# Sixteen key pages of the sample attention asked for on SyncE at the prompt attention's last scores, four more into a room of their own

## The chip, the core and the metric

The kernel runs on one core of a Trainium2 chip. The core has five engines with a queue of instructions each: PE (TensorE, matmuls and transposes), DVE (VectorE), ACT (ScalarE), POOL (GpSimd) and SP (SyncE, which here only issues DMAs), and 16 DMA engines that carry what the queues ask for. PEld is the load of a matmul's stationary operand. The metric is the device time of one execution in microseconds, the median of several; lower is better.

## The reference, cut to what matters

One step of a two-layer decoder for two groups of tokens that share all weights: a prompt of 512 tokens and a sample of 8 sequences with one new token each. The change touches one part of layer 0, the attention of the sample.

```
def nsa_sample(xn, kv_cmp_pages, kv_sel_pages, kv_win_buf, page_table, ...):
    past = page_table.shape[1] * PAGE_SIZE             # 8 pages of 128 rows, 1024 keys
    ...
    def gather_past(pages):
        return pages[page_table].reshape(b, past, 2, N_KV_HEADS, HEAD_DIM)
    ...
    sel_all = jnp.concatenate([gather_past(kv_sel_pages), sel_new], axis=1)
    win_all = jnp.concatenate([kv_win_buf, jnp.stack([k_w, v_w], axis=2)], axis=1)
    ...
    o = nsa_attend(q, q_rot, gates, pos, kc, vc, sel_blk[:, :, :, 0], sel_blk[:, :, :, 1],
                   win_all[:, :, 0], win_all[:, :, 1], kw_pos)
```

Each of the 8 sequences has 8 pages of selected-branch keys and 8 of values (a page is 128 rows of 256 f32, 128 KB), found through `page_table`, and one window of 512 keys and 512 values (512 KB each). Nothing of what is computed changes.

## The kernel before

The program is a row of blocks. At the end of a block every engine drains, reports to a barrier, and goes on when all five have reported; the instructions of the next block start behind it. Two neighbouring blocks matter.

**The prompt attention** (L2357 and on) works in units n = 0 to 39: scores on PE, exponents, scaling, transposes and products with the values. SP has nothing to compute there. It issues DMAs for the block that follows, each group behind a wait on how far the prompt attention has come (`scored`, `o_filled`, `c_turned`), because the rooms come free one after another.

**The sample attention** (`stage_sample_attention`, L2836 and on) takes the keys in 12 groups g of four transposed tiles: `group(n)` gives for turn n the parity j of the sequence, the part (2 is the window, 0 and 1 are the first and last four pages), the half a and the quarter q, so that the sequence is b = 2q + j. Groups 0 to 5 are the even sequences, 6 to 11 the odd ones. Each turn is four transposes into PSUM, a copy to `sa_kT`, and one of four products; the semaphore `turned` counts turns. Before group 8 PE waits for part 0 of the odd sequences, before group 10 for part 1 (`k_landed`). Then come softmax steps, and the products with the values (L2956), first for sequences 0 to 3 (bg = 0), then 4 to 7 (bg = 1); before each half PE waits for `v_landed` of its four sequences.

The values are loaded by `rows_values`, 9 DMAs a sequence (the window and 8 pages). Most land in rooms that keys held before, so they wait for `turned` to reach 8, 24, 32, 40 or 48 (`v_free`). SP loads sequences 0, 1, 4, 5; POOL 2, 3, 6, 7. Behind its last value page SP asks for the first weight tile of the next stage (`load_first_weights`, L2697, 2 MB into `w_first`).

A page's number comes from the table in SBUF. SP has read the numbers of its own sequences 0, 1, 4, 5 into registers before (`read_table`). For the other four, `early_keys` has SP read the number at the page (`table`, L2744: a TENSOR_LOAD and two register operations ahead of the DMA). Below, such a page is a table page, the other kind an own page.

The key pages of the odd sequences, `k_slots(1, part, q)`, are loaded so before: (1, 0, q=0) by SP at the end of the prompt attention; (1, 0, 2), (1, 1, 0), (1, 1, 2) by SP and (1, 0, 1), (1, 0, 3), (1, 1, 1), (1, 1, 3) by POOL at the start of the sample attention.

Of the kernel before, what the change touches and what calls it, by code (L numbers as in the profile page):

```python
# [19 lines left out]
P = 128  # L20
# [10 lines left out]
KVW = NKV * HD  # L31
# [56 lines left out]
class Core:  # L88


    def __init__(self, nc, ctx, dram):
        self.nc, self.ctx, self.dram, self.sems = nc, ctx, dram, []
        self.psum = ctx.enter_context(nc.psum_tensor("psum", [P, 8, 512], F32))
# [38 lines left out]
def columns(w):  # L132

    view = w.rearrange("(k p) n -> p k n", p=P)
    return lambda g, chunk: view[:, chunk * CK:(chunk + 1) * CK, g * NG:(g + 1) * NG]
# [2132 lines left out]
def stage_prompt_attention(c, cache):  # L2268
# [20 lines left out]
    scaled, turned = ([c.sem(f"att_{x}_{par}") for par in ("even", "odd")] for x in ("scaled", "turned"))  # L2289
    kept = [c.sem(f"att_kept_{half}") for half in ("first", "second")]  # L2290
    o_filled, o_kept = c.sem("att_o_filled"), c.sem("att_o_kept")
    with ExitStack() as mine:
# [64 lines left out]
        with nc.Block() as block:  # L2357
# [264 lines left out]
            @block.sync  # L2622
            def _(sp):
                cache.read_table(sp, "sp")
                sp.wait_ge(c.h_stored, 16)
                cache.first_selected(sp)
                sp.wait_ge(k_turned, 4)
                cache.first_windows(sp)
                sp.wait_ge(scored, 2 * NR)
                cache.window_keys(sp, 1, 0, 0)  # L2630
                sp.wait_ge(o_filled, 4)
                cache.early_keys(sp, 0, 1, 2, 0, 2)
                sp.wait_ge(scored, 4 * NR)
                cache.window_keys(sp, 1, 1, 1)
                sp.wait_ge(o_filled, 8)
                cache.early_keys(sp, 0, 1, 2, 2, 4)
                sp.wait_ge(c_turned, 3)
                cache.early_keys(sp, 0, 1, 0, 0, 4)
                cache.early_keys(sp, 0, 1, 1, 0, 2)
                sp.wait_ge(scored, 6 * NR)  # L2640
                cache.window_keys(sp, 1, 2, 0)
                sp.wait_ge(o_filled, 12)
                cache.early_keys(sp, 0, 1, 3, 0, 2)
                sp.wait_ge(c_turned, 4)
                cache.early_keys(sp, 0, 1, 1, 2, 4)
                sp.wait_ge(scored, NU)
                cache.window_keys(sp, 1, 3, 1)
                cache.early_keys(sp, 1, 0, 0, 0, 4)


NKC = PAST // P
# [43 lines left out]
def load_first_weights(c, sp):  # L2695

    sp.dma_start(c.w_first[:], columns(c.dram["nsa_w_o"][0])(0, 0)).then_inc(c.w_first_landed, 16)  # L2697


class SampleCache:  # L2700
# [5 lines left out]
    def __init__(self, c):  # L2706
        self.c, self.values = c, {}
        self.sel_pages = c.dram["cache_kv_sel"][0].rearrange("g t s h d -> g t (s h d)")
        self.win = c.dram["cache_kv_win"][0].rearrange("b (c t) s h d -> b t c (s h d)", t=P)
        self.k_landed = [[[c.sem(f"sa_k_landed_{j}_{part}_{e}") for e in ("sp", "pool")] for part in range(3)] for j in range(2)]  # L2710
        self.v_landed = [c.sem(f"sa_v_landed{b}") for b in range(NB)]
        self.kept_h = c.hT[:].rearrange("p k t -> p (k t)")[:, 0:16 * KVW].rearrange("p (s x) -> p s x", x=KVW)
        self.more = None

    def dead(self, q):

        row, half = ((0, 0), (0, 1), (1, 0), (2, 0))[q]
        return self.c.kv[:, 0:QT, row, half * KVW:(half + 1) * KVW]

    def k_slots(self, j, part, q):  # L2720

        if j == 0 and part == 2:
            return self.dead(q)
        if j == 0 and part == 0:
            return self.kept_h[:, 4 * q:4 * q + 4]
        at = 16 * {(0, 1): 0, (1, 2): 1, (1, 0): 2, (1, 1): 3}[j, part] + 4 * q
        return self.more[:, at:at + 4]

# [66 lines left out]
def stage_sample_attention(c, cache):  # L2795
# [11 lines left out]
    turned, kept, scored, s_done = c.sem("sa_turned"), [c.sem("sa_kept_act"), c.sem("sa_kept_dve")], c.sem("sa_scored"), c.sem("sa_scores_done")  # L2807
# [4 lines left out]
    with ExitStack() as mine:  # L2812
# [23 lines left out]
        with nc.Block() as block:  # L2836
            @block.sync
            def _(sp):
                cache.early_keys(sp, 0, 1, 3, 2, 4)
                cache.keys(sp, 1, 0, 2)  # L2840
                for q in (0, 2):
                    cache.keys(sp, 1, 1, q)
                for b in cache.OWN["sp"]:
                    cache.rows_values(sp, b, turned)
                load_first_weights(c, sp)

            @block.gpsimd
            def _(pool):
                for part in range(2):
                    for q in (1, 3):  # L2850
                        cache.keys(pool, 1, part, q)
                for b in cache.OWN["pool"]:
                    cache.rows_values(pool, b, turned)

# [1195 lines left out]
```

## Time and profile before

| | us |
|---|---|
| median of 3 runs | 1504.61 |
| lowest, highest | 1503.66, 1506.21 |
| the profiled execution, its own time | 1503.56 |
| its span, first to last instruction | 1501.9 |
| prompt attention ends (last PE instruction ends) | 397.0 |
| sample attention, PE's first to last instruction | 398.0 to 463.3 |

The span is read as a chain: PE is busy 97% of it, so a microsecond comes off the end only if PE loses it. The sample attention is one of the few places where PE has gaps that other engines or transfers decide. Times in the rows are from the start of the span. "Idle before" is how long the engine stood before an instruction, and the name behind the arrow is what released it; "issue" stands where the profile shows no releaser. A q behind an engine's name is its sequencer, which runs waits, register and DMA-issuing instructions.

### The profile page before, as it was taken

The numbers are of one execution on the slowest core, as the hardware profiler recorded it, in microseconds if no ns is written. First come the engines' busy times: TensorE is split into PE (matmuls) and PEld (weight loads), VectorE is DVE, ScalarE is ACT, GpSimd is POOL, SyncE is SP. The second block draws the span as 40 slices with busy tenths as digits, with TensorE's granted clock in tenths as the row PEclk, the third lists the DMA queues.
The fourth block names the chain that finished last, engine by engine and source line by source line (L and its number), as shares of the span: only waits on it lengthen the run. The fifth ranks groups of instructions, "written<-read, shape, count | busy, mean of one in ns | idle before, by whom it ended". The sixth has DMA issues, their size and how long they took to land. (4 is left out here: it accounts for less than half of the span.)

```text
span 1501.9 us, 25637 instructions
## 1 busy us (share of the span) xinstructions
PE 1459.0 (97%) x9697; PEld 1216.4 (81%) x9697; DVE 867.1 (58%) x1878; ACT 418.0 (28%) x1052; POOL 353.7 (24%) x478
## 2 busy tenths in 40 slices
PE   8999999899999999999999999899999999999998
PEld 7877799655557888888888888688888888888888
DVE  2755344788555795654767725661585556776513
ACT  3011333788520533324200001442531111000012
POOL 0000300467640369991000036380000000000000
PEclk9999999999999999999999999999999999999999
DMA  8345472221496445363344311602312222322201
GB/s 271 116 126 150 128 235 63 80 71 44 149 350 157 156 166 168 134 228 138 120 135 133 110 63 55 282 31 92 108 61 81 88 98 71 113 84 84 85 28 58
DMA packets 142893, 184.34 MB, mean 123 GB/s; under 512 B 31299, under 2 KB 101643, under 8 KB 141747
## 3 DMA queue, kind: packets, MB, share of 16 engines
q1 hardware_dynamic: 139634, 174.31, 35.4%
q0 software_dynamic: 3136, 8.39, 1.7%
q8 instruction: 77, 1.26, 0.3%
q14 instruction: 46, 0.37, 0.1%
HBM read 163.42 MB, written 29.69 MB: 129 GB/s over the span
## 5 line engine op out<-in xcount | busy, mean ns | idle before, releaser
L2619 POOL TENSOR_SCALAR att_p<-att_p,att_tot,gates 128x128 f32<-128x128 f32 (+3 forms) x128 | 79.1, 631 | 45.2 <-DVE att_tot L2541 44.6
L296 PE MATMUL psum<-xT,l_w 128*128 128x260 f32 x384 | 85.3, 383 | 2.0 <-PEq L113 1.8
L953 PE MATMUL psum<-xT,l_w 128*128 128x260 f32 x384 | 85.2, 383 | 1.6 <-PEq L113 1.6
L296 PEld LDWEIGHTS psum<-xT,l_w 128*128 128x128 f32 x384 | 72.8, 190 | 13.5 <-issue 2.4
L953 PEld LDWEIGHTS psum<-xT,l_w 128*128 128x128 f32 x384 | 72.8, 190 | 12.9 <-issue 1.8
L969 PE MATMUL psum<-l_up_t,l_w_sums 128*128 128x260 f32 x336 | 78.2, 382 | 0.0
L2145 PE MATMUL psum<-cmp_xt,cmp_w 64*128 64x256 f32 (+1 forms) x640 | 72.2, 362 | 0.3 <-DVE cmp_xt L2066 0.3
L969 PEld LDWEIGHTS psum<-l_up_t,l_w_sums 128*128 128x128 f32 x336 | 63.8, 190 | 9.8
L2592 ACT ACTIVATE att_p<-att_p,att_low 128x128 f32<-128x128 f32 (+3 forms) x128 | 70.4, 553 | 2.7 <-DVE att_low L2532 2.7
L1232 ACT ACTIVATE l_hidden<-l_tmp 128x260 f32<-128x260 f32 x64 | 26.6, 420 | 144.9 <-DVE l_tmp L1382 144.9
L2532 DVE CUSTOM_DVE_ANT_0 att_p<-psum,causal 128x128 f32<-128x128 f32 (+3 forms) x128 | 55.8, 487 | 18.7 <-PE psum L2367 17.9
L312 PE MATMUL psum<-xT,l_w 128*128 128x260 f32 x272 | 62.9, 382 | 0.0
L969 PE MATMUL psum<-xT,l_w 128*128 128x260 f32 x272 | 62.9, 382 | 0.0
L312 PE MATMUL psum<-l_up_t,l_up_w_sums 128*128 128x260 f32 x264 | 61.5, 382 | 0.0
L2145 PEld LDWEIGHTS psum<-cmp_xt,cmp_w 64*128 64x128 f32 x640 | 60.7, 187 | 0.6 <-DVE cmp_xt L2066 0.5
L969 PE MATMUL psum<-xT,l_w_sums 128*128 128x260 f32 x256 | 60.4, 382 | 0.0
L969 PEld LDWEIGHTS psum<-xT,l_w 128*128 128x128 f32 x272 | 51.7, 190 | 7.9
L1086 PE MATMUL psum<-l_hidden,l_w 128*128 128x260 f32 (+2 forms) x384 | 58.1, 311 | 0.0
L1715 PE MATMUL psum<-xT,proj_w 128*128 128x260 f32 x256 | 56.8, 383 | 0.7 <-DMA proj_w<-in_nsa_w_in 0.5
L312 PEld LDWEIGHTS psum<-xT,l_w 128*128 128x128 f32 x272 | 51.1, 190 | 7.5
L1086 PEld LDWEIGHTS psum<-l_hidden,l_w 128*128 128x128 f32 x384 | 53.8, 191 | 3.9
L455 PE MATMUL psum<-l_hidden,l_w 128*128 128x260 f32 x256 | 56.4, 382 | 0.0
(584 smaller groups left out, 3148.8 us busy)
## 6 DMA issues: line engine op xcount, KB each, us to landing
l_w<-in_mlp_w SPq DMA_DIRECT2D x16, 2048.0 KB, 8.0
l_w<-in_mlp_w SPq DMA_DIRECT2D x32, 1024.0 KB, 5.1
proj_w<-in_nsa_w_in SPq DMA_DIRECT2D x4, 2048.0 KB, 10.3
cmp_raw<-in_cache_kv_cmp SPq DMA_DIRECT2D x24, 256.0 KB, 3.0
xT<-in_cache_kv_cmp SPq DMA_DIRECT2D x24, 256.0 KB, 3.0
sa_more<-in_cache_kv_sel POOLq DMA_DIRECT2D x44, 128.0 KB, 6.6
sa_more<-in_cache_kv_sel SPq DMA_DIRECT2D x34, 128.0 KB, 8.0
hT<-in_cache_kv_cmp SPq DMA_DIRECT2D x16, 256.0 KB, 3.1
```

The lines of the kernel that those rows point to most:

```text
L296: mm = nc.tensor.matmul(ps[:, n % 8, 0:HALF], w[s][:, k, m * P:(m + 1) * P], src[:, kk, cols(h)], start=(kk == 0), stop=(kk == last))
L312: mm = nc.tensor.matmul(ps[:, bank, 0:HALF], left(k), right(k), start=(fresh and k == 0), stop=(ends and k == KC - 1))
L455: mm = nc.tensor.matmul(ps[:, LAST_BANKS[h, m], 0:HALF], wt[:, k, at:at + P], hid[:, kk, cols(h)], start=(kk == 0), stop=(kk == KF - 1))
L953: mm = nc.tensor.matmul(ps[:, n % 8, 0:HALF], w[s][:, k, m * P:(m + 1) * P], src[:, kk, cols(h)], start=(kk == 0), stop=(kk == last))
L969: mm = nc.tensor.matmul(ps[:, bank, 0:HALF], left(k), right(k), start=(fresh and k == 0), stop=(ends and k == KC - 1))
L1086: mm = nc.tensor.matmul(ps[:, LAST_BANKS[part][m], 0:width(part)], wt[:, k, at:at + P], hid[:, kk, PARTS[part]], start=(kk == 0), stop=(kk ...
L1232: nc.scalar.activation(hid[:, tile, cols(h)], tmp[:, i % 4], ACT.Square).then_inc(hid_done, 1)
L1715: mm = nc.tensor.matmul(ps[:, bank_of(step), 0:HALF], w[:, j, k, m * P:(m + 1) * P], c.xT[:, k, h * HALF:(h + 1) * HALF], start=(k == 0), ...
L2145: mm = nc.tensor.matmul(out, w1[z * HD:(z + 1) * HD, i % 2, t].rearrange("p r e -> p (r e)"), moving, start=(t == 0), stop=(t == STRIDE - 1))
L2532: nc.vector.tensor_tensor_reduce(pr[:, n % PR, par, at:at + w], ps[:, score_bank(n, par), at:at + w], c.causal[:, SEQ - w:SEQ], 1.0, 3e38, ...
L2592: nc.scalar.activation(pr[:, n % PR, par, at:at + w], pr[:, n % PR, par, at:at + w], ACT.Exp, scale=-1.0, bias=low[:, n % PR, u, par:par + ...
L2619: ve.tensor_scalar(pr[:, n % PR, par, at:at + w], pr[:, n % PR, par, at:at + w], tot[:, n % PR, u, par:par + 1], c.gates[:, i, gate:gate + ...
```

## The change

Three things.

At the end of the prompt attention SP asks for 16 pages, (1, 0, q) for q = 0, 2, 1, 3 behind the wait for the last scores, where it asked for the four of q = 0. And it asks near the block's start for the four pages of (1, 1, 0), into a new room `sa_spare`.

In the sample attention SP then has only (1, 1, 2) of the odd keys left, four pages in place of twelve, and POOL eight in place of sixteen.

`sa_spare` lies partly on `w_first`, so SP waits for `turned` to reach 45 (the last reading of the room) before it asks for the weight tile.

```
@@ first_windows, in the prompt attention @@
                 cache.first_windows(sp)
+                cache.early_keys(sp, 1, 1, 0, 0, 4)
                 sp.wait_ge(scored, 2 * NR)
...
                 sp.wait_ge(scored, NU)
                 cache.window_keys(sp, 1, 3, 1)
-                cache.early_keys(sp, 1, 0, 0, 0, 4)
+                for q in (0, 2, 1, 3):
+                    cache.early_keys(sp, 1, 0, q, 0, 4)
@@ SampleCache @@
+        self.spare = c.place("sa_spare", [P, 4, KVW], 222112 - 55488)
...
+        if (j, part, q) == (1, 1, 0):
+            return self.spare[:]
@@ stage_sample_attention, SP @@
                 cache.early_keys(sp, 0, 1, 3, 2, 4)
-                cache.keys(sp, 1, 0, 2)
-                for q in (0, 2):
-                    cache.keys(sp, 1, 1, q)
+                cache.keys(sp, 1, 1, 2)
                 for b in cache.OWN["sp"]:
                     cache.rows_values(sp, b, turned)
+                sp.wait_ge(turned, 45)
                 load_first_weights(c, sp)
@@ POOL @@
-                for part in range(2):
-                    for q in (1, 3):
-                        cache.keys(pool, 1, part, q)
+                for q in (1, 3):
+                    cache.keys(pool, 1, 1, q)
```

How this moves instructions, in the words of the built programs (a DMA row names what it fills and from what; ISA is the register work of the page's address; three or more like rows are cut to "..."):

SP, end of the prompt attention, before: four own pages, then the end of the block (L2357) and the barrier.

```order
L2762 DMA sa_early<-in_cache_kv_win 128x4x256 [waits att_scored]
L2780 ISA
L2780 DMA sa_early<-in_cache_kv_sel 128x256
...
L2357 UNCONDITIONAL_BRANCH
L2837 UNCONDITIONAL_BRANCH [waits barrier_Pool_Activation_PE_DVE_SP_release]
```

The same place in the changed program (L2785 is the old L2780, L2749 the old L2744): eight own pages (q = 0, 2), then eight that read the table first (q = 1, 3).

```order
L2767 DMA sa_early<-in_cache_kv_win 128x4x256 [waits att_scored]
L2785 ISA
L2785 DMA sa_early<-in_cache_kv_sel 128x256
...
L2749 TENSOR_LOAD pages
L2749 ISA x2
L2785 ISA
L2785 DMA sa_early<-in_cache_kv_sel 128x256
...
L2357 UNCONDITIONAL_BRANCH
L2842 UNCONDITIONAL_BRANCH [waits barrier_Pool_Activation_PE_DVE_SP_release]
```

Between the last scores and SP's report to the barrier now stand 16 page DMAs and 8 table reads, where there were 4 page DMAs.

SP, end of the sample attention, before: the weight tile straight behind the last value page.

```order
L2792 ISA [waits sa_turned]
L2792 DMA sa_more<-in_cache_kv_sel 128x256
...
L2697 DMA l_w_49<-in_nsa_w_o 128x8x512
L2836 UNCONDITIONAL_BRANCH
L235 UNCONDITIONAL_BRANCH [waits barrier_Pool_Activation_PE_DVE_SP_release]
```

And in the changed program:

```order
L2797 ISA [waits sa_turned]
L2797 DMA sa_more<-in_cache_kv_sel 128x256
...
L2699 DMA l_w_49<-in_nsa_w_o 128x8x512 [waits sa_turned]
L2841 UNCONDITIONAL_BRANCH
L235 UNCONDITIONAL_BRANCH [waits barrier_Pool_Activation_PE_DVE_SP_release]
```

The weight tile has a wait of its own now; nothing else stands behind it on SP in this block.

## Rows read from the trace of the kernel before

**Rows 1.** The page: busy time, share of the span, instructions.

```profile
PE 1459.0 (97%) x9697; PEld 1216.4 (81%) x9697; DVE 867.1 (58%) x1878; ACT 418.0 (28%) x1052; POOL 353.7 (24%) x478
```

**Rows 2.** Timeline of PE, 395 to 466 us: start, length, what, idle before.

```profile
395.90 1.13 PE L2412 MATMUL psum<-qT,attc_vcz 128*128 128x512 f32 x2
397.96 0.65 PE L2865 MATMUL psum<-kcs,qz 128*32 128x63 f32 x32 [0.93 <-PEq L2357]
...
405.93 1.99 PE L2887 MATMUL psum<-ident,hT 128*128 128x128 f32 x16
407.90 1.06 PE L2897 MATMUL psum<-sa_kT,qz 128*32 128x512 f32 x8
...
441.62 1.09 PE L2922 MATMUL psum<-ident,qz 128*128 128x128 f32 x8 [1.89 <-DVE qz L3004]
...
449.52 0.39 PE L2956 MATMUL psum<-sa_more,sa_kT 128*16 128x256 f32 x2
451.31 0.62 PE L2956 MATMUL psum<-vcs,causal 63*16 63x256 f32 x8 [1.40 <-issue]
...
465.08 35.30 PE L296 MATMUL psum<-xT,l_w 128*128 128x260 f32 x160 [1.75 <-PEq L113]
```

**Rows 3.** Instructions of L2357, the barrier at the prompt attention's end: duration, start.

```profile
L2357 SPq DRAIN  x1: 122/122/122, 388.3 to 388.3; - x1
L2357 POOLq DRAIN  x1: 2282/2282/2282, 389.6 to 389.6; - x1
L2357 ACTq DRAIN  x1: 614/614/614, 397.1 to 397.1; - x1
```

**Rows 4.** Waits of SP's queue, 285 to 399 us: total, times, longest.

```profile
SPq L2357 <- PEq L2357: 9.4, 1, 9.4
```

**Rows 5.** Timeline of SP, 285 to 399 us.

```profile
296.56 2.08 SPq L2762 DMA_DIRECT2D kv<-in_cache_kv_win  x4
300.42 0.37 SPq L2762 DMA_DIRECT2D sa_early<-in_cache_kv_win  x1
317.01 0.89 SPq L2780 DMA_DIRECT2D sa_early<-in_cache_kv_sel  x2
...
374.49 3.96 SPq L2780 DMA_DIRECT2D sa_early<-in_cache_kv_sel  x4
385.78 0.39 SPq L2762 DMA_DIRECT2D sa_early<-in_cache_kv_win  x1
386.36 1.91 SPq L2780 DMA_DIRECT2D sa_early<-in_cache_kv_sel  x4
```

**Rows 6.** SP's page DMAs, 386 to 389 us (four own pages): duration, first and last start.

```profile
L2780 SPq DMA_DIRECT2D sa_early<-in_cache_kv_sel x4: 333/333/368, 386.4 to 387.9; - x4
```

**Rows 7.** SP's table reads, 347 to 352 us (two), then 373 to 379 us (four).

```profile
L2744 SPq TENSOR_LOAD <-pages x2: 265/269/273, 349.5 to 350.6; - x2
...
L2744 SPq TENSOR_LOAD <-pages x4: 267/268/276, 373.8 to 377.4; - x4
L2744 SPq FUSED_REGOPS  x4: 152/154/159, 374.1 to 377.7; - x4
```

**Rows 8.** Page DMAs of L2759, SP (eight own, eight table pages), first and last start.

```profile
L2759 SPq DMA_DIRECT2D hT<-in_cache_kv_sel x16: 332/333/651, 283.2 to 296.2; - x16
```

**Rows 9.** Windows: us, busy of five engines, granted clock, DMA share, GB/s.

```profile
392.00:396.00 4.00, 4.00 (x43) 2.22 (x41) 0.69 (x1) 0.58 (x1) 0.00 (x0) 1.00 0.00 0
408.00:412.00 4.00, 4.00 (x34) 2.15 (x34) 2.09 (x4) 1.26 (x3) 3.13 (x6) 1.00 1.06 354
448.00:452.00 4.00, 2.60 (x48) 1.09 (x44) 1.68 (x4) 0.00 (x0) 0.00 (x0) 1.00 1.07 371
```

**Rows 10.** Page DMAs of L2792 in tile `sa_more`: all of SP; then SP, POOL from 430 us.

```profile
L2792 SPq DMA_DIRECT2D sa_more<-in_cache_kv_sel x20: 333/654/1489, 408.2 to 441.3; - x20
...
L2792 POOL DMA_DIRECT2D sa_more<-in_cache_kv_sel x15: 537/537/877, 429.9 to 442.2; - x15
L2792 SPq DMA_DIRECT2D sa_more<-in_cache_kv_sel x13: 333/416/1315, 429.9 to 441.3; - x13
```

**Rows 11.** Timeline of POOL, 411 to 462 us.

```profile
428.66 0.76 POOL L2789 DMA_DIRECT2D sa_more<-in_cache_kv_win  x1 [4.55 <-PE psum L2887]
...
435.02 2.32 POOL L2792 DMA_DIRECT2D sa_more<-in_cache_kv_sel  x4 [3.44 <-PE psum L2887]
...
438.08 4.67 POOL L2792 DMA_DIRECT2D sa_more<-in_cache_kv_sel  x8
```

**Rows 12.** DMAs in issue 442.6 to 443 us: count, KB each, us to landing.

```profile
l_w<-in_nsa_w_o SPq DMA_DIRECT2D x1, 2048.0 KB, 13.9
sa_more<-in_cache_kv_sel SPq DMA_DIRECT2D x1, 128.0 KB, 9.9
sa_more<-in_cache_kv_sel POOLq DMA_DIRECT2D x1, 128.0 KB, 7.2
```

**Rows 13.** DMA queues, 444 to 446 us: packets, MB, share.

```profile
q1 hardware_dynamic: 192, 0.18, 29.2%
q0 software_dynamic: 191, 0.52, 76.7%
```

**Rows 14.** Windows around a gap of PE in the prompt attention, columns as rows 9.

```profile
278.00:280.00 2.00, 0.31 (x4) 0.00 (x0) 1.93 (x7) 1.74 (x9) 1.50 (x2) 1.00 0.00 0
280.00:281.00 1.00, 0.73 (x2) 0.47 (x4) 1.00 (x8) 1.00 (x5) 0.00 (x0) 0.67 0.00 0
281.00:283.00 2.00, 2.00 (x20) 1.12 (x16) 2.00 (x6) 1.04 (x5) 1.91 (x3) 0.50 0.00 0
283.00:284.00 1.00, 0.60 (x6) 0.38 (x4) 1.00 (x3) 0.97 (x2) 0.78 (x2) 0.62 0.00 0
```

**Rows 15.** Timeline of PE, 276 to 294 us.

```profile
280.27 2.04 PE L2367 MATMUL psum<-att_kT,qrT 64*128 64x512 f32 x4 [1.96 <-DVE att_low L2532]
...
287.83 1.13 PE L2367 MATMUL psum<-att_kT,qrT 64*128 64x512 f32 x4 [2.56 <-DVE att_low L2532]
```

## The prediction

> **What bounds the kernel now.** I read the page's busy times first: PE is busy 97% of the span [rows 1], so only what PE loses or wins counts. Then PE's timeline through the two blocks that the change touches [rows 2]. Between the prompt attention and the sample attention PE stands 0.93 us, released by the barrier. The twelve groups of key turns are back to back: a group of 16 transposes and its products takes 1.99 + 1.06 us less a little overlap, 405.93 to 408.90, and the next ones look alike, none with a wait for a transfer. So the keys that the change asks for earlier keep nobody waiting now. Two gaps follow: 1.89 us for a DVE chain, and 1.40 us at 449.91 before the first product of bg = 1, put down to "issue". For that gap I looked at the transfers, since PE waits there for `v_landed` of sequences 4 to 7. SP's last value page was asked for at 441.3 [rows 10] and landed 9.9 us later [rows 12], at 451.2; PE goes on at 451.31. POOL's last page was asked for at 442.2 and landed 7.2 us later, at 449.4. So the 1.40 us belong to SP's pages of sequence 5, which sat in a full queue: the DMA engines carry about 350 GB/s without a pause there [rows 9]. Last I looked at who reaches the barrier when [rows 3]: SP drains at 388.3 and stands 9.4 us [rows 4]; ACT is the last, its drain ends at 397.1 + 0.61 = 397.7.
>
> **What the change removes.** Sixteen pages of 128 KB, 2.1 MB, leave the sample attention, 2.1 / 350 GB/s = 6.0 us of transfer. SP's value pages no longer stand behind eight key pages. The last eight wait for `turned` = 40, which POOL's row dates at 428.66 [rows 11]; asked for at 0.5 us each they are out by 433 and, even at today's 9.9 us, in by 443. So SP's pages fall away as the reason for the gap. What is late next is POOL's last page. POOL's queue is unchanged from `turned` = 24 on: its last 13 DMAs still wait for `turned` = 48 and go out from 435.0 to 442.75 [rows 11]. With its 7.2 us it is in at 449.4, half a microsecond before PE asks. The gain is the whole 1.40 us. It cannot be more: before the gap PE runs without one from 441.62, behind it PE and DVE work on as before, and the next stage's first tile landed at 442.7 + 13.9 = 456.6 [rows 12], 8 us before its first product at 465.08 [rows 2].
>
> **What the change adds at the end of the prompt attention.** This is the term that decides. Behind the wait for the last scores (released at 385.78) SP had one window and four own pages, and was through at 388.3 [rows 5]. Now 12 more pages stand there, and the barrier behind them is one that PE waits for. An own page costs (387.9 − 386.4) / 3 = 0.51 us from start to start [rows 6]. A table page costs more: in the row at 374.49 four of them take 3.96 us; less the last DMA's own 0.33 that is 3.63 / 3 = 1.21 us [rows 5]. Rows 8 give a second value: 15 steps in 13.0 us, seven of them own, so (13.0 − 7 × 0.51) / 8 = 1.18. Two table reads in the middle of the block start 349.5 and 350.6, 1.1 us apart [rows 7]. I take 1.15, between the last and the other two. The additions are 4 × 0.51 + 8 × 1.15 = 2.0 + 9.2 = 11.2 us. SP's last DMA starts at 387.9 + 11.2 = 399.1, ends at 399.5, and its drain of 0.12 us at 399.6. The barrier would have opened at 397.7, so SP is now the last and PE, with everybody, starts the sample attention 1.9 us later. With 1.1 us a table page SP is done at 399.2 and 1.5 us late, with 1.21 at 400.1 and 2.4 late.
>
> A narrower reading is possible from the durations alone: a table read is 0.27 us and its register work 0.15 [rows 7], so a table page would be 0.51 + 0.44 = 0.95 us, SP done at 398.0 and 0.3 us late. I keep 0.3 as the lower bound and don't take it as the value, because the starts show a gap behind each read that no row accounts for. The Trainium skill (DMA: Bandwidth & Descriptors, "Latency and other measured facts") puts the floor of a `tensor_load` at about 600 ns. As an estimate by that page, a table page would be 0.51 + 0.60 = 1.11 us and SP 1.6 us late; the row's 0.27 us duration speaks against the page's figure, the distance of the starts for it.
>
> **The rest.** The four pages of (1, 1, 0) go out near the block's start, behind the kv windows (issued 296.56 to 298.64). They are own pages: 4 × 0.51 = 2.0 us to 300.7. The next DMA, now at 300.42, slips by 0.3 us, and SP's next wait ends at 317.0 [rows 5], so it costs nothing; without that pause it would cost 2.0. The 12 more pages at the end cross an idle DMA system (share 0.00 from 392 to 396 [rows 9]). POOL issues 8 key pages instead of 16 and then waits for `turned` = 8; nothing of its is on the path. The new wait for `turned` = 45 has nothing behind it on SP but the weight tile. PE passes 45 turns about 432, before SP is through with its value pages, so the tile goes out around 434 and not at 442.7. Its 2.1 MB now share the engines with POOL's last 2.1 MB. With at most 1.0 MB of sequence 5 still outstanding that is 5.2 MB / 350 GB/s = 15 us from 434.4, so everything is in by 449.4 at the latest, still before 449.9. All these times slide together with the late barrier.
>
> **The sum.** +1.9 (SP late at the barrier) − 1.4 (gap before bg = 1) = +0.5 us. Everything else is 0. The profiled execution would go from 1503.56 to 1504.1; it lies 1.05 us below the median, which is the execution's luck, so I add the difference to the median: 1504.61 + 0.5 = 1505.1.
>
> **Rivals.**
>
> B, SP is in time. Table pages at the end of the block cost 0.9 us or less: 8 × 0.9 + 2.0 ends SP at 397.6. Then only the gap goes: 1504.61 − 1.4 = 1503.2. For it: the durations [rows 7]. Against it: three stretches of SP's queue [rows 5, 7, 8].
>
> C, the pause lets TensorE's clock fall. PE's pause at the barrier grows from 0.93 to about 2.8 us. The trace has a pause of 1.96 us before 280.27 [rows 15] behind which the granted clock is 0.67, 0.50 and 0.62 (its lower level, 1.2 GHz, for the middle two) until 284 [rows 14]: 0.33 + 1.0 + 0.38 = 1.7 us of full clock lost. But behind the pause of 2.56 us before 287.83 nothing fell, and before this barrier PE has been busy without a pause for 5 us. If it falls: +0.5 + 1.7 = +2.2, 1506.8. The Trainium skill (TensorE: Matmul & The Clock Gate, "Part 1: The HAM clock gate") ties the level to how busy the engine has just been and halves the clock after idleness; the two pauses here show both outcomes.
>
> D, the gap stays. The weight tile takes the place of SP's pages beside POOL's. The two queues take turns by packet (192 against 191 packets [rows 13]), POOL's being the larger now, 0.52 against 0.18 MB; if the tile's packets are larger than page rows, POOL's share falls. POOL has half a microsecond to lose. Then the 1.4 us stay: +1.9, 1506.5. Against it: the 15 us bound above, and SP's queue being empty far earlier.
>
> E, the other side: SP is held up by a full queue. In the sample attention a page DMA takes 0.65 us in the median, 1.49 at most, instead of 0.33 [rows 10]. If the twelve added ones were held up so, SP would be 12 × 0.32 = 3.8 us later still: +0.5 + 3.8 = +4.3, 1508.9. It decides from the point where pages are asked for faster than they are carried, one in 0.37 us at 350 GB/s. Own pages come one in 0.51 us, table pages slower, so it should not.
>
> **How the numbers follow.** Forecast 0.58, B 0.10, C 0.14, D 0.12, E 0.06. The forecast's own range is 1503.5 (0.3 us late) to 1505.6 (2.4 late) by the bounds of the table page, and 1502.9 to 1506.5 with half the spread of the three runs of before (1503.66 to 1506.21). The range reaches to B's and D's times and a little past C: 1502.6 to 1507.2; E lies outside, with the edges of B and C. A measurement of this kernel tells about 0.2%, 3.0 us, from no change. Faster by that needs B and 1.6 us more: 0.03. Slower needs E, or C and D together: 0.08. Within: 0.89.
>
> **What would show it.** In the changed profile: SP's last page DMA before the barrier starts at 399.1 and its drain, not ACT's, is the last; POOL and ACT wait for it. PE's gap before L2868 (the old L2865) is about 2.8 us, not 0.93. The gap of 1.40 before the first product of bg = 1 is gone, and the products of bg = 0 and 1 follow each other. From the start of the sample attention to its last PE instruction it is 65.3 − 1.4 = 63.9 us. The granted clock stays at 1.00 in the windows from 400 on. The forecast is wrong if SP reaches the barrier before 397.7 (B), if the clock reads 0.5 behind the pause (C), if a gap remains in L2959 (D, the old L2956), or if page DMAs of L2785 last over 0.4 us at the block's end (E).

## The result: slower by 0.3%, and the profile after

The changed kernel takes 1508.55 us in the median of 10 runs (1505.91 to 1513.76); the kernel before, in 10 runs beside it, 1505.38 (1503.61 to 1507.79). The ratio is 1.0029 with a 95% interval of 1.0017 to 1.0041, that is 4.4 us (2.6 to 6.2). I had forecast +0.5 us, 1505.1, with a range up to 1507.2. A second set on another chip gave 1508.76 against 1505.17, ratio 1.0024 (1.0014 to 1.0034).

The profiled execution is one of the slowest: 1513.76 us, a span of 1512.1. So its 10.2 us over the profile before are not the change's price; its single steps are what can be read. PE's timeline in it, to be held against [rows 2] (start, length, what, idle before):

```profile
395.32 1.12 PE L2412 MATMUL psum<-qT,attc_vcz 128*128 128x512 f32 x2
399.63 1.07 PE L2868 MATMUL psum<-kcs,qz 128*32 128x63 f32 x32 [3.19 <-PEq L2357]
...
401.44 5.04 PE L2890 MATMUL psum<-ident,kv 128*128 128x128 f32 x24
...
446.07 1.16 PE L2925 MATMUL psum<-ident,qz 128*128 128x128 f32 x8 [1.89 <-DVE qz L3007]
...
447.37 1.05 PE L2959 MATMUL psum<-vcs,causal 63*16 63x256 f32 x8
...
459.06 0.62 PE L2959 MATMUL psum<-vcs,causal 63*16 63x256 f32 x8
```

Three things differ. PE's pause at the barrier is 3.19 us, it was 0.93. The transposes of the first six key turns take 5.04 us; in the kernel before they took 2.97:

```profile
399.07 2.97 PE L2887 MATMUL psum<-ident,kv 128*128 128x128 f32 x24
```

And bg = 0 of the value products takes 11.7 us (447.37 to 459.06), where it took 7.2 and a gap of 1.40. The barrier's own rows, against [rows 3] (duration, start), and what SP did before it, against [rows 5]:

```profile
L2357 ACTq DRAIN  x1: 616/616/616, 396.5 to 396.5; - x1
L2357 SPq DRAIN  x1: 123/123/123, 399.2 to 399.2; - x1
```

```profile
385.76 13.42 SPq L2785 DMA_DIRECT2D sa_early<-in_cache_kv_sel  x16
```

SP is the last now, done at 399.3 where ACT is done at 397.1: 2.2 us. The sixteen pages take 13.42 us. One of the first three is a page DMA that lasts 1.10 us instead of 0.33 (shortest, median and longest, first and last start):

```profile
L2785 SPq DMA_DIRECT2D sa_early<-in_cache_kv_sel x16: 332/333/1103, 385.8 to 398.9; - x16
```

Less these 0.77 us, the last DMA's 0.33 and seven own steps of 0.51 that is 8.75 / 8 = 1.09 us a table page. The windows of PE, against [rows 9] (us, busy of five engines, granted clock, DMA share, GB/s), say what the slow stretches are:

```profile
400.00:404.00 4.00, 4.00 (x104) 3.98 (x96) 1.33 (x5) 0.59 (x1) 3.47 (x7) 0.50 0.66 200
...
408.00:412.00 4.00, 4.00 (x36) 2.89 (x35) 1.88 (x3) 2.10 (x6) 2.88 (x5) 1.00 1.07 357
...
420.00:424.00 4.00, 4.00 (x34) 2.76 (x32) 1.58 (x3) 1.76 (x3) 2.78 (x5) 1.00 0.49 145
...
448.00:452.00 4.00, 4.00 (x40) 1.27 (x40) 0.84 (x3) 0.00 (x0) 0.00 (x0) 0.50 1.03 362
```

The granted clock is 0.50, the level of 1.2 GHz, behind the long pause and again behind the pause of 1.89 us. From 420 to 424 the DMA engines are half idle (share 0.49, 1.08 in the kernel before): with fewer keys to fetch, the queues have at that time nothing more to carry.

### The profile page after: what moved, and what is told of

It reads as the page before. It is cut to its first block and busy times, and to the rows that moved or that the text cites. A ratio compares the mean times of both kernels' runs of the same rounds, so it can differ in the third digit from the quotient of the medians.

```text
span 1512.1 us, 25661 instructions
## 1 busy us (share of the span) xinstructions
PE 1468.7 (97%) x9697; PEld 1221.0 (81%) x9697; DVE 867.5 (57%) x1878; ACT 418.4 (28%) x1052; POOL 350.0 (23%) x470
## 5 line engine op out<-in xcount | busy, mean ns | idle before, releaser
L953 PE MATMUL psum<-xT,l_w 128*128 128x260 f32 x384 | 86.9, 388 | 2.0 <-PEq L113 2.0
L296 PE MATMUL psum<-xT,l_w 128*128 128x260 f32 x384 | 85.3, 383 | 2.0 <-PEq L113 1.8
L953 PEld LDWEIGHTS psum<-xT,l_w 128*128 128x128 f32 x384 | 74.0, 193 | 13.7 <-issue 2.1
L296 PEld LDWEIGHTS psum<-xT,l_w 128*128 128x128 f32 x384 | 72.8, 190 | 13.5 <-issue 2.4
```

The costliest lines, as they stand in the source:

```text
L296: mm = nc.tensor.matmul(ps[:, n % 8, 0:HALF], w[s][:, k, m * P:(m + 1) * P], src[:, kk, cols(h)], start=(kk == 0), stop=(kk == last))
L953: mm = nc.tensor.matmul(ps[:, n % 8, 0:HALF], w[s][:, k, m * P:(m + 1) * P], src[:, kk, cols(h)], start=(kk == 0), stop=(kk == last))
```

## The experiments

All times below come with those of the kernel before on the same chip: medians 1504.63, 1504.79, 1505.17 and 1504.98 us in the four sets. Medians of different rows come from different chips, and of 8 to 12 runs each; where they and the ratios tell different sizes, the ratio with its interval is the one to hold to. The last four columns are read from one profile of each kernel. "Pause" is PE's idle time at the prompt attention's end. "Block" is the time from PE's first instruction of the sample attention to its first of the next stage (L296). "bg = 0" is the time from the first value product of bg = 0 to that of bg = 1. "L953" is PE's idle time at a later barrier. A star marks the profiles in which the granted clock fell behind the 1.89 us pause.

| kernel | median us | ratio to before (95%) | pause | block | bg = 0 | L953 |
|---|---|---|---|---|---|---|
| before, first profile | | | 0.9 | 67.1 | 8.6 | 1.6 |
| before, second profile | | | 0.9 | 67.3 | 8.7* | 1.6 |
| changed, first set | 1508.55 | 1.0029 (1.0017 to 1.0041) | 3.2 | 73.2 | 11.7* | 2.0 |
| own_only | 1505.00 | 1.0000 (0.9991 to 1.0008) | 0.9 | 67.3 | 8.7* | 1.6 |
| read_ahead | 1507.15 | 1.0010 (1.0000 to 1.0020) | 0.9 | 67.3 | 8.7* | 2.0 |
| late_sync | 1507.73 | 1.0014 (1.0001 to 1.0027) | 2.6 | 71.6 | 10.1* | 1.6 |
| awake | 1508.07 | 1.0018 (1.0010 to 1.0027) | 0.5 | 68.8 | 10.0* | 2.0 |
| own_fill | 1504.15 | 0.9995 (0.9987 to 1.0004) | 0.9 | 66.2 | 7.6 | 1.6 |
| before_fill | 1504.38 | 0.9999 (0.9990 to 1.0008) | 0.9 | 71.3 | 9.5 | 1.6 |
| pool_pad | 1504.60 | 0.9999 (0.9990 to 1.0008) | 0.9 | 67.3 | 8.7* | 1.6 |
| pad_fill | 1504.82 | 0.9996 (0.9987 to 1.0004) | 0.9 | 66.9 | 8.4 | 1.6 |
| changed_pad | 1508.40 | 1.0022 (1.0012 to 1.0033) | 3.2 | 71.3 | 9.8* | 1.6 |
| pad_early | 1504.58 | 1.0000 (0.9991 to 1.0010) | 0.9 | 67.3 | 8.7* | 1.6 |
| changed_again | 1508.76 | 1.0024 (1.0014 to 1.0034) | 2.4 | 68.2 | 8.4 | 2.0 |
| tile_late | 1503.86 | 0.9990 (0.9980 to 1.0000) | 0.9 | 65.7 | 7.1 | 1.6 |
| changed_tile_late | 1508.02 | 1.0020 (1.0011 to 1.0029) | 2.4 | 67.0 | 7.1 | 2.0 |
| own_tile_late | 1503.28 | 0.9987 (0.9978 to 0.9996) | 0.9 | 65.6 | 7.1 | 1.6 |

**own_only** undoes the table pages:

```
-                for q in (0, 2, 1, 3):
+                for q in (0, 2):
                     cache.early_keys(sp, 1, 0, q, 0, 4)
...
-                for q in (1, 3):
-                    cache.keys(pool, 1, 1, q)
+                for part in range(2):
+                    for q in (1, 3):
+                        cache.keys(pool, 1, part, q)
```

> The changed kernel with the eight table pages put back: at the prompt attention's end SP asks for the eight own pages (1, 0, 0) and (1, 0, 2) only; (1, 0, 1) and (1, 0, 3) are POOL's again in the sample attention. Theory (the loss is SP's lateness at the barrier, and what PE's long pause there does to the clock): SP is through near 390.5, the pause before L2868 is 0.9 us again, the clock stays 1.00 at 400 to 406, and the value products have no 1.4 us gap; 1.4 us faster than before, about 0.999 of it. Rival (moving the keys early disturbs the sample attention itself, by another phase of the transfers or by the weight tile's wait): as slow as the changed kernel, 3 us over before, with the pause at 0.9.

Measured 1505.00, no different from before: the loss is gone, the expected gain of 1.4 us did not come.

**read_ahead** keeps all sixteen pages, and reads the table where SP waits anyway:

```
+                cache.ahead = {b: [cache.table(sp, b, j) for j in range(4)] for b in (3, 7)}
                 sp.wait_ge(scored, NU)
```

> The changed kernel, all sixteen pages asked for at the same place, but SP reads the eight table numbers of sequences 3 and 7 before it waits for the last scores, where it stands idle. Theory (table reads behind the last wait make SP late): 16 pages x 0.51 us from 386.4 end at 394.5, before ACT's 397.7; the pause is 0.9 us, the clock at 400 to 406 is 1.00, the gap before bg = 1 is gone: 1.4 us faster than before. Rival (the sixteen DMAs or their transfers hold up the block's end): the pause stays near 3 us and the time near the changed kernel's, 3 us over before.

Its SP drains at 394.6, in time; the pause is 0.9 and the clock at 400 to 406 is 1.00, all as expected. Yet the median is 1507.15, 2.1 over own_only (by the ratios 1.5, with intervals that overlap). Neither reading allowed for that, and the profile names a place that I had not looked at: PE stands 2.0 us before L953, 560 us behind the edit, instead of 1.6.

**late_sync** moves nothing, and makes SP late:

```
                 cache.early_keys(sp, 1, 0, 0, 0, 4)
+                for i in range(18):
+                    cache.table(sp, 3, i % 8)
```

> The kernel before with nothing moved, but SP reads 18 table numbers that nobody uses behind its last page DMA at the prompt attention's end, about 0.6 us each, so that it comes to the barrier about as late as in the changed kernel. Theory: this alone makes the loss. Pause before L2865 about 3 us, about 2 us later from there, the gap of 1.4 us stays: +2 us where the clock holds, and +4 to +9 in executions in which it falls behind the pauses; median 3 to 5 us over before. Rival (the loss comes from the moved transfers): 2 us over before and the clock never below 1.00 between 398 and 460.

Measured +3.1 us in the median, by the ratio 2.1 (0.2 to 4.1), 1503.99 to 1513.14. Its profile has SP's drain at 400.1 (ACT is done at 398.5), a pause of 2.57 us, and low clock from 400 to 407. Being late is enough for the pause and the low clock, without any moved key, and for at least a part of the loss.

**awake** is the changed kernel with PE busy during SP's lateness:

```
                         if m >= 0 and m % NR in LAST:
                             values(m, part)
+                keep_awake(c, 0, 9)
```

> The changed kernel with nine matmuls on the identity (2.2 us) as PE's last work in the prompt attention, so that PE's pause at the late barrier is about 1 us; nothing else differs. It tells the wait from the clock. Theory (the pause lets the clock fall): no window below 1.00 between 398 and 410, and the time is the sum of the prediction, +0.5 to +1 us over before, without executions 5 to 9 us over. Rival (the clock falls for another reason, or the wait is the whole loss): same median as the changed kernel, 3 us over before, with the same spread.

The clock stayed at 1.00 at 400 to 410, as the theory said. The slowest run is 1511.1 us where the changed kernel's is 1513.8. But the median is 1508.07, not 1505.5, and its ratio can't be told from the changed kernel's. The block of its profile says what the theory left out: 68.8 us against 67.3, because the clock fell behind the 1.89 us pause (windows near 0.50 from 447 to 454) and bg = 0 took 10.0 us. SP is late here too (done at 402.3, ACT at 400.8). The clock behind the barrier is shown by the profiles; that its repair brings time back is not shown by this median.

**own_fill** and **before_fill** fill the pause of 1.89 us in the softmax chain, in own_only and in the kernel before:

```
+                keep_awake(c, 5, 7)
                 pe.wait_ge(weighed[2], 1)
```

> own_only with seven matmuls on the identity (1.7 us) put into PE's pause of 1.89 us before the transposes of the selected weights. In own_only's profile the clock stood at its lower level from 447 to 451 behind that pause and ate the 1.4 us that the missing gap gives. Theory (the clock eats the gain): with the pause filled the clock stays 1.00 through the value products and own_fill is 1 to 3 us faster than own_only (median 1502 to 1504). Rival (the gain was never there, or PE's matmuls delay the transposes): the same as own_only or slower, 1505.

> The kernel before with the same seven matmuls in the same pause and nothing else. Theory: the kernel before loses its clock there in some executions too, so it gains up to 1.5 us by the filling; its gap of 1.4 us before bg = 1 stays, so own_fill is 1.4 us faster than this kernel. Rival (only the moved keys make the clock fall there): no change against before, 1504.6.

own_fill is 0.9 under own_only in the median, inside the intervals; before_fill does not tell itself from before. Its profile has full clock through bg = 0 and then a gap of 2.34 us, longer than the 1.40 of [rows 2], and the clock fell behind that gap, at 455:

```profile
454.11 0.62 PE L2957 MATMUL psum<-vcs,causal 63*16 63x256 f32 x8 [2.34 <-issue]
```

In own_fill the clock held through the value products, and its profile shows what stands there, with the keys moved, without the cover of a low clock (start, length, what, idle before):

```profile
453.10 0.62 PE L2961 MATMUL psum<-vcs,causal 63*16 63x256 f32 x8 [0.49 <-DMA sa_more<-in_cache_kv_sel]
```

A gap of 0.49 us is left, released by a value page.

**before_again** is a second profile of the kernel before.

> The kernel before, unchanged, for a second profile of it. Theory (the clock falls behind PE's pauses by chance, before as after): some stretches of low clock at 280 to 294, 442 to 456 or 944 to 960 differ in place and length from the first profile's, and the time follows them. Rival (the kernel before is free of it between 400 and 460 by construction): again none in the sample attention.

It took 1505.51 us, and differs where the theory said: low clock from 444 to 450 (windows 0.82, 0.50, 0.83), and no gap before bg = 1 at all. But the time does not follow from that: of the 2.0 us by which its span is longer, 1.8 stand before the sample attention begins (399.74 against 397.96), and the block is 67.3 us against 67.1.

```profile
444.53 0.62 PE L2956 MATMUL psum<-vcs,causal 63*16 63x256 f32 x8
...
453.25 0.62 PE L2956 MATMUL psum<-vcs,causal 63*16 63x256 f32 x8
```

From the first product of bg = 0 to that of bg = 1 are 8.7 us here, and 8.6 in [rows 2]. The slow clock and the gap cover each other: where the clock falls behind the 1.89 us pause, the pages are there in time.

**pool_pad** and **pad_early** give POOL's program its old length in read_ahead, with eight reads that nobody uses, at two different places:

```
                 for q in (1, 3):
                     cache.keys(pool, 1, 1, q)
+                for i in range(8):
+                    cache.table(pool, 3, i)
```

> read_ahead with eight table reads that nobody uses on POOL in the sample attention, which gives POOL's program the length it had before (24 instructions fewer in the changed kernel). In the changed kernel, read_ahead and awake PE stood 2.0 us at the barrier before L953 instead of 1.6, with POOL's drain the last, and in two of three the clock fell behind it. Theory (the shorter program of POOL shifts where its instructions are fetched): that pause is 1.6 again, no low clock near 1030, and the median is 1.5 to 2 us below read_ahead's 1507.2, about as own_only's 1505.0. Rival (the sixteen early pages or the spare room cost it): the pause stays 2.0 and the median 1507.

> read_ahead with the eight unused table reads of POOL at the end of its work in the prompt attention, where it stands 7 us idle, instead of in the sample attention. Theory (POOL's length ahead of the later barrier decides, not what the reads do to its page requests): like pool_pad, pause before L953 of 1.6 and median near 1504.6. Rival (the reads helped by delaying POOL's value pages): like read_ahead, pause 2.0 and median 1507.

Both expectations held, 1504.60 and 1504.58; by the ratios the two lie 1.7 and 1.5 us under read_ahead, with intervals that overlap its own. PE's wait (total, times, longest) at the later barrier in read_ahead, then in pool_pad:

```profile
PE psum L953 <- PEq L113: 2.0, 1, 2.0
```

```profile
PE psum L953 <- PEq L113: 1.6, 1, 1.6
```

**changed_pad** and **changed_again** put this to the changed kernel.

> The changed kernel itself with the eight unused table reads on POOL, nothing else. It leaves the late SyncE alone of the two causes. Theory (two causes add up): PE's pause before L953 is 1.6 again, the pause at the prompt attention's end stays near 3.1, and the median lies 1.5 to 2.5 us under the changed kernel's 1508.6 and 2 us over before. Rival (POOL's length matters only in read_ahead): the median stays at 1508.6.

> The changed kernel, unchanged, for a second profile on the chip of these runs and for its time beside changed_pad's. Theory: SP's drain is the last at the prompt attention's end by 2 us again, the clock falls behind the pause of 3 us, which is longer than any other pause of the run, and the pause before L953 is 2.0; 3 to 5 us over before. Rival (the first profile was an unlucky execution): no low clock between 398 and 410, within 2 us of before.

changed_pad's pause before L953 is 1.6, but its median of 1508.40 lies only 0.4 under changed_again's 1508.76: the expected 1.5 to 2.5 us did not come. changed_again shows the late drain (400.7 against ACT's 398.7), a low clock from 400 to 405, and a thing that settles a rival. Its value products ran at full clock, and PE still stood:

```profile
455.57 0.62 PE L2959 MATMUL psum<-vcs,causal 63*16 63x256 f32 x8 [1.23 <-DMA sa_more<-in_cache_kv_sel]
```

Its DMA queues from 444 to 446 us (packets, MB, share), against [rows 13]:

```profile
q0 software_dynamic: 150, 0.42, 59.6%
q1 hardware_dynamic: 156, 0.30, 42.2%
```

POOL's queue still gets every second packet, but the other queue's packets are the weight tile's now, 0.30 MB / 156 = 1.9 KB instead of 0.9, and POOL moves 0.42 MB in the time of 0.52. What was carried from the tile's issue at 437.4 to the end of PE's gap at 455.6:

```profile
DMA packets 3089, 6.14 MB, mean 337 GB/s; under 512 B 419, under 2 KB 1312, under 8 KB 3087
```

**pad_fill** joins the three mendings.

> pool_pad with the seven matmuls in the 1.89 us pause: all sixteen pages early, the table numbers read ahead, POOL's program as long as before, the pause filled. Theory: everything the change could give is left, the missing gap of 1.4 us, and its costs are gone: median 1503.0 to 1504.0, 0.7 to 1.5 us under before, and no low clock between 398 and 460. Rival (the early pages cost something of their own): over own_fill's 1504.2.

1504.82, over the expected range; its profile has full clock from 398 to 460, and a gap of 1.22 us before bg = 1, again released by a page of POOL's. The theory failed. Whether its rival held is not shown: 1504.82 is over own_fill's 1504.15, but the ratios, 0.9996 and 0.9995, are the same.

**tile_late**, **changed_tile_late** and **own_tile_late** move the tile behind the value pages, in pad_fill, the changed kernel and own_fill:

```
                 sp.wait_ge(turned, 45)
+                sp.wait_ge(v_landed[7], 16 * (NPAGE + 1))
                 load_first_weights(c, sp)
```

> pad_fill with one more wait: SP asks for the next stage's weight tile only when all nine value DMAs of sequence 7, POOL's last, have landed. In pad_fill, own_fill and changed_again, whose value products ran at full clock, PE still stood 1.2, 0.5 and 1.2 us before bg = 1, released by a value page of POOL's. Theory (the tile, asked for about 8 us earlier than before, takes every second packet beside POOL's pages): without it POOL's pages land 2 us or more earlier, the gap is 0, and the median falls by 0.5 to 1.2 us against pad_fill's 1504.8; the tile lands near 456, 9 us before it is read. Rival (POOL's pages are late by their own issue, or the tile becomes late): the gap stays at 1.2, or PE waits before L296 for the tile.

> The changed kernel with that wait alone. It leaves the late SyncE, the clock and POOL's length, and takes the tile away from the value pages. Theory: no gap before bg = 1 in an execution at full clock; of the 3.6 us over before some 0.5 to 1.2 go, median 1507.5. Rival (the gap is hidden in most executions by a low clock in bg = 0): no change in the median, 1508.5.

> own_fill with that wait alone: the eight own pages early, the pause filled, the tile behind the value pages. Theory: the gap of 0.49 us of own_fill's profile is gone, median 1503.3 to 1504.0, the fastest of the kernels here, 0.7 to 1.5 us under before. Rival: with more keys left to load in the sample attention SP's own value pages are what is late, as in the kernel before: the gap stays and the median is own_fill's 1504.2.

In all three profiles the gap is gone. PE in own_tile_late, then its DMAs in issue from 440 to 446 us:

```profile
444.24 0.62 PE L2962 MATMUL psum<-vcs,causal 63*16 63x256 f32 x8
...
451.32 0.62 PE L2962 MATMUL psum<-vcs,causal 63*16 63x256 f32 x8
...
465.08 15.14 PE L296 MATMUL psum<-xT,l_w 128*128 128x260 f32 x68 [1.75 <-PEq L113]
```

```profile
sa_more<-in_cache_kv_sel POOLq DMA_DIRECT2D x8, 128.0 KB, 5.5
```

bg = 0 takes 7.1 us, with no idle behind it. From PE's first instruction of the block (399.45) to L296 it is 65.6 us, 67.1 in [rows 2]: the 1.4 us that the prediction had booked, and 0.1 more. POOL's pages land in 5.5 us, where changed_again's last eight took 7.9 in the median, and own_fill's 7.5. tile_late's median is 1.0 under pad_fill's, own_tile_late's 0.9 under own_fill's, changed_tile_late's 0.7 under changed_again's; by the ratios it is 0.9, 1.2 and 0.6, and in each pair the intervals overlap. So it is the profiles, not the medians, that show what the tile does. own_tile_late is the fastest kernel here, 0.13% (0.04 to 0.22) under the kernel before.

## Why the prediction was wrong, point by point

**SP late at the barrier: right.** +1.9 us forecast. End of SP's drain less the end of ACT's is 399.3 − 397.1 = 2.2 us in the first profile, 401.7 − 399.5 = 2.2 in changed_pad and 400.8 − 399.3 = 1.5 in changed_again. The table page was taken a little too dear: 1.10 us in changed_again (12.68 − 0.33 − 7 × 0.51 = 8.78, by 8) and 1.09 in the first profile, where 1.15 was taken. With 1.1 the prediction had 1.5 us. The other 0.8 in two profiles are no table reads: one page DMA of the first three lasted 1.10 us there (1.18 in changed_pad), while in changed_again, changed_tile_late and awake none is over 0.37. That is the sign I had named for E, at a fifth of E's price; what held that one DMA up is open. That the forecast of 1.9 lies between the two cases is partly luck. The estimate by the Trainium skill (DMA: Bandwidth & Descriptors, "Latency and other measured facts"), 1.11, agrees with the 1.10 measured; the reading from bare durations, 0.95, was off.

**The clock, rival C: taken for unlikely, and it is the rule.** I gave it 0.14 because one of two pauses of this length in the trace left the clock alone. Of the five profiles with a pause of 2.4 us or more at this barrier (changed twice, late_sync, changed_pad, changed_tile_late) all five have the clock at 0.50 behind it; of the twelve with 0.9 or less none, and one of these, awake, has SP as late as the others. Its price can be read from PE's first instruction of the block to the first value product: 44.8 us in [rows 2] and in ten more of the twelve (45.1 in awake), 46.1 and 46.2 in two of the five, 47.7 in three. That is 1.3 to 2.9 us, where I had 1.7. The failed step is the weighing, not the mechanism: two pauses are too few to take odds from, and the one that cost nothing had no claim to be the typical one. The Trainium skill (TensorE: Matmul & The Clock Gate, "Part 1: The HAM clock gate") has the clock halved when TensorE has been idle; these profiles agree in the level, 0.50 behind all five pauses.

**The second fall, behind the 1.89 us pause: in no term.** It cost more where SP was late. In the five profiles of kernels with a punctual SP in which the clock fell there, bg = 0 took 8.7 us, about as long as with the gap of [rows 2]. In the four with a late SP (the changed kernel's first, late_sync, changed_pad, awake) it took 11.7, 10.1, 9.8 and 10.0, that is 1.1 to 3.0 us more, because the clock stayed low longer. In awake this came without a fall at the barrier. Why the low stretch is longer there is open. It is the largest part of the loss in the first profile that the prediction put at nothing.

**The gap before bg = 1, −1.4: wrong, rival D came true.** The failed step is the bound "everything is in by 449.4 at the latest". It counted 5.2 MB and left bytes out. In changed_again the tile was asked for at 437.4, in a block that starts 3 us later (442.7 in the kernel before), and 6.1 MB were carried from there until PE went on. Besides the tile's 2.1 and the 2.1 of POOL's last 13 DMAs that is 1.9 MB where I had at most 1.0 of sequence 5: POOL's window and four pages asked for behind `turned` = 40 (at 433.1 to 436.0 here, landing in 7.0 and 6.7 us; at 428.66 in [rows 11]) were still under way. With 6.1 MB the same bound reads 434.4 + 17.4 = 451.8 us, 2 us behind 449.9 instead of half a microsecond before it. The way two queues share did the rest: the tile brought packets of twice the size, and POOL's last page, asked for at 446.6, landed 8.8 us later instead of 7.2. changed_again has 1.23 us of the 1.40 left, pad_fill 1.22. tile_late and own_tile_late show that it is the tile; how much its bytes and how much its packets' size did was not separated. I had written down D's mechanism and then let a byte count with an item missing overrule it.

**That the gap is always there: wrong too, and in no rival.** The kernel before shows it in one profile of two, and where the clock was held, in before_fill, it is 2.34 us. Behind the 1.89 us pause the clock fell in 9 of the 12 profiles in which the pause is unfilled, in before_again too; bg = 0 then takes 8.7 us or more and the pages come in time. So 1.4 us were there to be won only in some executions. That is why own_only's profile, with neither a late SP nor low clock at 400, has won nothing (67.3 us), and why own_tile_late, with the pause filled and the tile held back, did. Filling the pause alone won nothing in the kernel before; holding back the tile in the changed kernel alone did not show in the median either.

**"POOL has nothing on the path": wrong by 0.4 us and more.** A POOL program shorter by eight page requests lengthens PE's pause before L953 from 1.6 to 2.0 us, in all five profiles of kernels with it and in none of the other twelve. It was not in any list of mine. In two of those five profiles, the first of the changed kernel and read_ahead's, the clock was low behind it (windows near 1030), in none of the twelve; from L953 to the end of the span it is then 478.0 us instead of 476.3, 1.7 more. The median of read_ahead is 2.5 us over those of its two mended forms, 1.5 to 1.7 by the ratios, with intervals that overlap: the price in the median is not measured well. In the changed kernel the mending did not show (0.4 us, changed_pad). What in POOL's program does it is open: eight unused reads mend it at either of two places (pad_early), and fetching of instructions, the guess of pool_pad's expectation, is seen in no view here.

**The rest held.** The four pages for the spare room cost nothing, the twelve more transfers met idle DMA engines, E came true for one page DMA of sixteen in two of five profiles and not as a full queue, the wait for `turned` = 45 held up nothing, and the tile came in time. That the median, 1508.55, lies beside E's 1508.9 is chance. The band of 1502.9 to 1506.5 was worked out wrong (half of 2.55 us on either side of 1503.5 to 1505.6 gives 1502.2 to 1506.9); the stated range does not hang on it.

**The sum again**, by profile, against the first one of before. changed_again, in which the second fall did not come: 1.5 (SP) + 1.3 (clock) − 0.2 (gap) + 0.4 (L953) = 3.0 us. The first profile: 2.3 (SP, by PE's pause) + 2.9 (clock) + 3.1 (bg = 0 at low clock, less the gap) + 0.4 (L953) + 1.7 (clock behind it) = 10.4, and it was one of the slowest runs. The median, 4.4 (2.6 to 6.2), lies between these executions; how often each fall comes in the runs that were not profiled is not known.

## What to carry to other kernels

A barrier makes every engine's queue a part of the critical path: count what stands behind the last wait of the idlest engine, register loads included, before giving it work, and put those reads ahead of the wait (read_ahead has the pause back at 0.9 us). A pause of PE costs its length and the slower work behind it, so price both, and expect a gain of a microsecond in a stall to be covered by the clock in some executions. When a transfer is moved forward, ask which small transfers it will share the engines with, packet by packet, and count every transfer that is still under way, those of the other queue too, before trusting a bound by bytes.

## What the runs showed of the hardware that I had not expected

The clock fell behind a pause of 1.89 us in 9 of 12 profiles and behind one of 2.4 to 3.2 us in 5 of 5, and stood at 0.50 for 3 to 11 us after. Five profiles with the 1.89 us pause filled down to 0.3 had no fall at that place; in before_fill it fell some 11 us later, behind a gap of 2.3 us before bg = 1. The kernel before spreads over 1502.7 to 1510.1 us in 126 runs. The clock is a part of that and, as far as the runs show, not most of it: the runs' times and their mean granted clocks correlate at −0.49, a quarter of the variance. PE reaches the barrier at the prompt attention's end at 396.4 to 400.8 us in the sixteen profiles whose PE has the same work up to there (all but awake), a spread as large as the effects told here.

Eight page requests fewer on POOL moved a barrier 560 us later by 0.4 us. POOL's drain there starts 1.0 us behind DVE's instead of 0.6 (read_ahead, then pool_pad; duration, start):

```profile
L113 DVEq DRAIN  x1: 136/136/136, 1024.9 to 1024.9; - x1
L113 POOLq DRAIN  x1: 40/40/40, 1025.9 to 1025.9; - x1
```

```profile
L113 DVEq DRAIN  x1: 137/137/137, 1028.3 to 1028.3; - x1
L113 POOLq DRAIN  x1: 40/40/40, 1028.9 to 1028.9; - x1
```

Two DMA queues that were both full took turns packet by packet, with page rows and with the tile's larger packets in the second queue (150 to 156 above, 191 to 192 in [rows 13]). The Trainium skill says that a DMA engine takes turns between its queues by packets (DMA: Bandwidth & Descriptors, "Queues, rings and completion order"), and the trace agrees. When the other queue's packets doubled, POOL's queue moved 0.42 MB in 2 us instead of 0.52.
